# First array carries the per-channel columns; spins in one block; upper 64 partitions on ScalarE's DMA queue

## The chip, the cores and the metric

One core of one Trainium2 chip runs the kernel. The metric is the device time of one launch in microseconds (us): the median of the runs shown. Changes are told in us and as a share of that time.

## What is computed

The reference is one layer of a hybrid encoder on 1024 frames of 1024 channels, all in float32:

```
h = rms_norm(x, norm1_g)
[u | q | k | v] = h @ w_in            (widths 512, 512, 128, 128)
a = pooling mixer(u), scaled by pool_scale
b = sliding-window attention(q, k, v) with q_norm_g, k_norm_g, sinks
x = x + concat(a, b) @ w_out
x = x + squared_relu(rms_norm(x, norm2_g) @ w_up) @ w_down
```

The part that the change touches is the very start: the projection of the first two tiles of 128 frames to k, v and q, which needs `norm1_g` as a scale of the rows of `w_in`.

## The kernel before, in words

**Precision.** Each float32 product is made as three TensorE products of rounded operands: high x high, low x high, high x low. The high part of an operand is its value rounded to fp32r, written by a copy on ScalarE; the low part is the value less the high part, written by a subtraction on VectorE. So nothing can be multiplied before ScalarE has written a high part, and nothing with a low part before VectorE has followed. For the weights both engines multiply by `g1`, the columns of `norm1_g` (one value per partition and k).

**Stages.** The frames are 8 tiles of 128, the 1024 input channels are 8 blocks `k` of 128. The program goes through projections and mixers (to about 180 us), the up projection and the down projection. Each engine has its own list of instructions, written out by hand; semaphores tie them together.

**The start, engine by engine** (line numbers of the profile):

- SP issues the loads. Three arrays come first (L416): `first_0` (tile 0's channels of k = 0, 1, and the k, v weights of k = 0, 1; 128 x 768 words), `first_1` (the same for tile 1, tile 0's k = 2, 3, the weights of k = 2, 3; 128 x 1024), `first_2` (tile 1's k = 2, 3 and the q weights of k = 0; 128 x 768). The q weights of k = 1 to 3 (L355), the second halves of x (L340), and the other k, v weights (L352) follow.
- ScalarE issues one load of its own (L883): `columns`, 18 rows of 128 words, which hold `norm1_g`, `pool_scale`, the q and k gains and the sinks as rows. It makes two slices of the attention bias (L881) and then the high parts in the order of the table `FIRST`: x of tile 0 (L662, `x_first_high`), k, v weights 0 and 1 (L693, `split_w_kv`), x of tile 1 (L662), tile 0's second pair (L666), weights 2 and 3 (L693), tile 1's second pair (L666), q weights 0 to 3 (L698).
- TensorE waits for a tile of zeros, multiplies it with itself 11 times ("spins", L1589: products whose result nobody reads), turns `columns` into 18 columns (L1775, a transpose through the array), spins 5 times, and then goes through the k, v products of k = 0 to 3 (L1581, 24 products of 256 columns, `project_first_kv`), with 2, 2 and 1 spins between them, and the q products (L1619 with high weights, L1623 with low ones, 512 columns each).
- VectorE makes the distance table and four slices of the bias (L1322, L1324), copies the turned columns out of PSUM to `per_row` (L1328), which both engines need as `g1`, and makes the low parts in ScalarE's order (L1055, L1060, L1112).

`first_hi` and `first_lo` count the high and low parts done; `first_count(kind, i)` is the place of a part in `FIRST`.

The list of TensorE at this place is this:

```python
            pe.wait_ge(setup_pool, 1)
            spin(11)
            pe.wait_ge(setup_pool, 4)
            pe.wait_ge(cols_in, 16)
            nc.tensor.transpose(bank[QT_B][:, 0:N_COLS], cols_rows[0:N_COLS, :], ...)
            spin(5)
            project_first_kv()
            project_first_q(range(KH), range(2))
```

Of the kernel before, what the change touches and what calls it, by code (L numbers as in the profile page):

```python
# [8 lines left out]
ACT = mybir.ActivationFunctionType  # L9
# [7 lines left out]
def hybrid_trunk(nc, x, x_T, columns, first_0, first_1, first_2, w_kv, w_q, w_u, pool_w, w_out, norm2_g, w_up, w_down, out):  # L17
# [33 lines left out]
    with ExitStack() as ctx:  # L51
# [100 lines left out]
        per_row = small(N_COLS)  # L152
        g1, pool_sc = per_row[:, 0:KT], per_row[:, KT:KT + GROUPS]
# [45 lines left out]
        cols_in, constants_in, x_tok_in = sem("cols_in"), sem("constants_in"), sem("x_tok_in")  # L199
# [19 lines left out]
        cols_turned = sem("cols_turned")  # L219
# [41 lines left out]
        FIRST = ([("x", 0), ("kv", 0), ("kv", 1), ("x", 1), ("kv", 2), ("kv", 3)] + [("q", k) for k in range(KH)]  # L261
                 + [("kv", k) for k in range(KH, KT)] + [("q", k) for k in range(KH, KT)])

        def first_count(kind, i):

            return FIRST.index((kind, i)) + 1

# [8 lines left out]
        COLS_READY = 1 + PAIRS + 1  # L276

# [60 lines left out]
        def _(sp):  # L338
# [76 lines left out]
            for i, piece in enumerate((first_0, first_1, first_2)):  # L415
                sp.dma_start(first_stage[i], piece).then_inc(first_in[i], 16)  # L416
# [9 lines left out]
            sp.wait_ge(first_lo, first_count("q", 0))  # L426
# [14 lines left out]
            sp.wait_ge(first_lo, len(FIRST))  # L441
# [203 lines left out]
        def _(sc):  # L645
# [14 lines left out]
            def x_first_high(t):  # L660
                sc.wait_ge(first_in[t], 16)
                nc.scalar.activation(act(HI, 0, t)[:, 0:2, :], x_first[t], ACT.Copy).then_inc(first_hi, 1)  # L662
# [60 lines left out]
            def copy_kv(t):  # L723
# [3 lines left out]
                else:  # L727
                    sc.wait_ge(first_lo, len(FIRST))
# [154 lines left out]
            sc.dma_start(cols_rows[0:N_COLS, :], columns).then_inc(cols_in, 16)  # L883
# [168 lines left out]
        def _(dve):  # L1052
            def x_first_low(t):
                dve.wait_ge(first_hi, first_count("x", t))
# [272 lines left out]
            dve.wait_ge(cols_turned, 1)  # L1327
            step(nc.vector.tensor_copy(per_row, bank[QT_B][:, 0:N_COLS]))  # L1328
# [19 lines left out]
            dve.wait_ge(first_lo, len(FIRST))  # L1348
# [196 lines left out]
        def _(pe):  # L1545
# [19 lines left out]
            def first_kv(t, k, x_part, w_part):  # L1565

                if (x_part, w_part) == (HI, HI):
                    if k < 2:
                        pe.wait_ge(first_hi, first_count("x", t))
# [3 lines left out]
                elif x_part == LO:  # L1573
                    if k < 2:
                        pe.wait_ge(first_lo, first_count("x", t))
                    else:
                        pe.wait_ge(xT_lo, xT_count(t, k // KH))
                else:
                    pe.wait_ge(first_lo, first_count("kv", k))
# [422 lines left out]
```

## Time and profile before

| | |
|---|---|
| median of 3 runs | 861.8 us (861.65 to 862.2) |
| the profiled execution, its own time | 862.25 us |
| its span, first to last instruction | 860.4 us |
| TensorE busy in the span | 856.7 us |
| VectorE, ScalarE, GpSimd busy | 541.7, 417.8, 232.1 us |

How to read it: a row of the timeline gives the start of a group of equal instructions, the time from its first start to its last end, the engine (PE is TensorE's matmul, PEld its weight load; DVE is VectorE, ACT ScalarE, POOL GpSimd, SPq and ACTq the engines' DMA issues), the line, the operation with what it writes and reads, and how many there are. Idle time before it and what ended it stand in brackets. Every product has one weight load, and the loads start one after the other at the pace of the products; so the start of one PEld row less that of the row before, by the number of loads in it, is the time of one product. The start of a PE row lies some 0.2 to 0.3 us behind its load.

### The profile page before, as it was taken

What the parts mean: (1) busy time and instruction counts of PE and PEld (TensorE: products, weight loads), DVE (VectorE), ACT (ScalarE), POOL (GpSimd) and SP (SyncE); (2) the same over time, 40 slices, a digit from 0 to 9 for tenths busy, and PEclk for the clock granted to TensorE, in tenths of its full rate; (3) what the DMA queues carried; (4) which work ended last, traced back from release to release, by engine and by line L of the source; (5) the groups of instructions that cost most, each with busy time, mean ns of one, the idle gap of its engine ahead of it and who ended that gap; (6) DMA issues with size and microseconds to landing.
All of it is one profiled execution on the core that took longest, in us unless ns stands there. A gap on an engine that the chain in (4) does not pass through costs nothing.

```text
span 860.4 us, 10823 instructions
## 1 busy us (share of the span) xinstructions
PE 856.7 (100%) x4068; PEld 710.8 (83%) x4068; DVE 541.7 (63%) x750; ACT 417.8 (49%) x737; POOL 232.1 (27%) x194
## 2 busy tenths in 40 slices
PE   9999999999999999999999999999999999999998
PEld 8888888888888888888888888888888888888887
DVE  7788588844477766656666566458745464646463
ACT  8875446632157555555555555534333333333330
POOL 1421202010141222244322223005543004444440
PEclk9999999999999999999999999999999999999999
DMA  9431013651011743355543332899742453342422
GB/s 353 174 107 66 26 26 73 221 196 50 32 42 50 240 165 134 135 177 177 168 153 135 135 136 97 307 373 363 268 167 95 166 190 120 103 138 100 143 98 74
DMA packets 67519, 128.37 MB, mean 149 GB/s; under 512 B 3578, under 2 KB 20236, under 8 KB 67468
## 3 DMA queue, kind: packets, MB, share of 16 engines
q1 hardware_dynamic: 67296, 127.55, 42.6%
q8 instruction: 32, 0.52, 0.2%
q14 instruction: 20, 0.16, 0.1%
q10 hardware_dynamic: 171, 0.14, 0.0%
HBM read 89.92 MB, written 37.75 MB: 148 GB/s over the span
## 4 chain that ended last, share of the span: by engine, by line
PE 100%; DVE 0%; POOL 0%; issue 0%; POOLq 0%
PE bank L1548 31%; PE bank L1549 31%; PE bank L1550 31%; PE bank L1751 1%; PE bank L1767 1%; PE bank L1561 1%; PE bank L1720 1%; PE bank L1619 1%; PE bank L1589 1%; PE bank L1581 1%; PE bank L1700 0%; PE bank L1623 0%; PE bank L1921 0%; PE bank L1926 0%; PE bank L1713 0%; PE bank L1704 0%
## 5 line engine op out<-in xcount | busy, mean ns | idle before, releaser
L1548 PE MATMUL bank<-b_op,s_op 128*128 128x512 f32 x446 | 173.2, 388 | 0.0
L1549 PE MATMUL bank<-b_op,s_op 128*128 128x512 f32 x446 | 173.1, 388 | 0.0
L1550 PE MATMUL bank<-b_op,s_op 128*128 128x512 f32 x446 | 173.1, 388 | 0.0
L1295 DVE TENSOR_TENSOR s_op<-s_in,s_op 128x1024 fp32r<-128x1024 f32 x56 | 74.4, 1329 | 126.9 <-ACT s_op L870 126.8
L634 POOL TENSOR_TENSOR b_sum<-d_raw,d_raw 128x1024 f32<-128x1024 f32 x40 | 96.9, 2422 | 201.1 <-DVE b_op L1299 201.1
L870 ACT ACTIVATE s_op<-s_in 128x1024 fp32r<-128x1024 f32 x56 | 59.4, 1060 | 177.3 <-PE bank L1550 148.8
L1256 DVE TENSOR_TENSOR ring<-raw,ring 128x512 fp32r<-128x512 f32 x96 | 88.3, 934 | 30.7 <-ACT ring L818 29.1
L1548 PE MATMUL bank<-xs,ring 128*128 128x512 f32 x256 | 99.7, 389 | 0.0
L1550 PE MATMUL bank<-xs,ring 128*128 128x512 f32 x256 | 99.6, 389 | 0.0
L1549 PE MATMUL bank<-xs,ring 128*128 128x512 f32 x256 | 99.6, 389 | 0.0
L1548 PEld LDWEIGHTS bank<-b_op,s_op 128*128 128x128 f32 x446 | 83.7, 188 | 17.5 <-DVE b_op L1299 0.3
L1550 PEld LDWEIGHTS bank<-b_op,s_op 128*128 128x128 f32 x446 | 83.7, 188 | 17.4
L1549 PEld LDWEIGHTS bank<-b_op,s_op 128*128 128x128 f32 x446 | 83.7, 188 | 17.1
L1548 PE MATMUL bank<-wgt,xs 128*128 128x512 f32 (+1 forms) x232 | 86.9, 374 | 0.0
L1550 PE MATMUL bank<-wgt,xs 128*128 128x512 f32 (+1 forms) x232 | 85.0, 366 | 0.0
L1549 PE MATMUL bank<-wgt,xs 128*128 128x512 f32 (+1 forms) x232 | 84.9, 366 | 0.0
L1548 PE MATMUL bank<-t_M,ring 128*128 128x512 f32 x192 | 74.7, 389 | 0.0
L1549 PE MATMUL bank<-t_M,ring 128*128 128x512 f32 x192 | 74.7, 389 | 0.0
L1550 PE MATMUL bank<-t_M,ring 128*128 128x512 f32 x192 | 74.7, 389 | 0.0
L593 POOL TENSOR_TENSOR raw<-raw 128x512 f32<-128x512 f32 x16 | 26.6, 1660 | 166.7 <-DVE ring L1256 166.6
L818 ACT ACTIVATE ring<-raw 128x512 fp32r<-128x512 f32 x96 | 59.2, 620 | 23.1 <-POOL raw L593 20.9
L1550 PEld LDWEIGHTS bank<-xs,ring 128*128 128x128 f32 x256 | 48.0, 188 | 10.0
(174 smaller groups left out, 1434.3 us busy)
## 6 DMA issues: line engine op xcount, KB each, us to landing
s_in<-h_keep SPq DMA_DIRECT2D x56, 512.0 KB, 3.8
h_keep<-h_set SPq DMA_DIRECT2D x16, 1280.0 KB, 5.1
raw<-in_w_up SPq DMA_DIRECT2D x16, 1024.0 KB, 5.7
d_raw<-in_w_down SPq DMA_DIRECT2D x32, 512.0 KB, 7.8
mem<-in_x SPq DMA_DIRECT2D x16, 512.0 KB, 5.2
h_keep<-h_set SPq DMA_DIRECT2D x16, 512.0 KB, 4.0
x_keep<-mem SPq DMA_DIRECT2D x8, 512.0 KB, 2.9
mem<-x_keep SPq DMA_DIRECT2D x8, 512.0 KB, 6.3
```

The source lines that it names most:

```text
L593: nc.gpsimd.tensor_tensor(out=w12, in0=w12, in1=w11, op=ALU.subtract).then_inc(w_four_ready, 1)
L634: nc.gpsimd.tensor_tensor(out=b_sum[G % 2], in0=group_rows(qa, g), in1=group_rows(qb, g), op=op).then_inc(b_summed, 1)
L818: nc.scalar.activation(ring[n % 6][:, HI], weight_block(n), ACT.Copy).then_inc(w_hi, 1)
L870: nc.scalar.activation(s_op[G % 3][:, HI], s_in[G % 3], ACT.Copy).then_inc(op_hi, 1)
L1256: nc.vector.tensor_tensor(out=ring[n % 6][:, LO], in0=weight_block(n), in1=ring[n % 6][:, HI].bitcast(F32), op=ALU.subtract).then_inc(w_lo, 1)
L1295: nc.vector.tensor_tensor(out=s_op[G % 3][:, LO], in0=s_in[G % 3], in1=s_op[G % 3][:, HI].bitcast(F32), op=ALU.subtract).then_inc(op_lo, 1)
L1548: nc.tensor.matmul(out_ap, lhs[HI], rhs[HI], start=first, stop=False, skip_group_check=chained)
L1549: nc.tensor.matmul(out_ap, lhs[HI], rhs[LO], start=False, stop=False, skip_group_check=chained)
L1550: return nc.tensor.matmul(out_ap, lhs[LO], rhs[HI], start=False, stop=last, skip_group_check=chained)
L1561: last = nc.tensor.transpose(xt_bank(T, i)[:, k * P:(k + 1) * P], x_norm[:, (4 * i + k) * P:(4 * i + k + 1) * P], ident)
L1581: last = nc.tensor.matmul(bank[KV_B[t]][:, 0:KV_W], act(x_part, k // KH, t)[:, k % KH, :], w_qkv_s[:, k, w_part, KV_COLS], start=k == 0 an ...
L1589: nc.tensor.matmul(bank[OUT_B][:, 0:2 * P], spin_tile[:, 0:P], spin_tile, start=True, stop=True)
```

## The change

The 18 columns come as columns: the host lays them behind the data of `first_0`, in 32 more words per partition (18 used), so that array is 128 x 800 words. The load of `columns`, the transpose and the copy out of PSUM are gone; VectorE copies the staged columns to `per_row` for later use, and the first two weight splits on ScalarE read them where they landed. `first_0` is loaded in two parts: partitions 0 to 63 from SP, 64 to 127 from ScalarE's queue, both counted by `first_in[0]`, now to 32. The high part of tile 0's x moves from ScalarE to VectorE (a copy with rounding, semaphore `x0_first_hi`), so ScalarE begins with the weights. TensorE spins 15 times in one block and not at all between products, and the 24 k, v products and the first q products stand in another order: the loop over k is outside, tile 1's low-x products of k = 2, 3 are put between the q products of k = 0.

```diff
-        cols_rows = view(a_junk + 2 * P, P)
-
-        a_first = [a_A, a_A + 3 * KV_W, a_A + 7 * KV_W]
-        first_stage = [view(a, w) for a, w in zip(a_first, (3 * KV_W, 4 * KV_W, 3 * KV_W))]
+
+        W_FIRST = (3 * KV_W + 32, 4 * KV_W, 3 * KV_W)
+        a_first = [a_A + sum(W_FIRST[:i]) for i in range(3)]
+        first_stage = [view(a, w) for a, w in zip(a_first, W_FIRST)]
...
+        staged_cols = view(a_first[0] + 3 * KV_W, N_COLS)
...
-        FIRST = ([("x", 0), ("kv", 0), ("kv", 1), ("x", 1), ("kv", 2), ("kv", 3)] + [("q", k) for k in range(KH)]
+        FIRST = ([("kv", 0), ("kv", 1), ("x", 1), ("kv", 2), ("kv", 3)] + [("q", k) for k in range(KH)]
...
+            return 1 if (kind, i) == ("x", 0) else first_count(kind, i) + 1
...
+        FIRST_LANDED = 32
...
-            for i, piece in enumerate((first_0, first_1, first_2)):
-                sp.dma_start(first_stage[i], piece).then_inc(first_in[i], 16)
+            sp.dma_start(first_stage[0][0:HD, :], first_0[0:HD, :]).then_inc(first_in[0], 16)
+            sp.dma_start(first_stage[1], first_1).then_inc(first_in[1], 16)
+            sp.dma_start(first_stage[2], first_2).then_inc(first_in[2], 16)
...
-                sc.wait_ge(w_kv_in[k // 2], 16)
+                sc.wait_ge(w_kv_in[k // 2], FIRST_LANDED if k < 2 else 16)
                 nc.scalar.activation(w_qkv_s[:, k, HI, KV_COLS], w_kv_stage[k // 2][:, k % 2, :], ACT.Copy,
-                                     scale=g1[:, k:k + 1]).then_inc(first_hi, 1)
+                                     scale=(staged_cols if k < 2 else g1)[:, k:k + 1]).then_inc(first_hi, 1)
...
-            sc.dma_start(cols_rows[0:N_COLS, :], columns).then_inc(cols_in, 16)
+            sc.dma_start(first_stage[0][HD:P, :], first_0[HD:P, :]).then_inc(first_in[0], 16)
             sc.wait_ge(setup_dve, 1)
             slope_rows(0)
             slope_rows(1)
-            x_first_high(0)
-            sc.wait_ge(setup_dve, COLS_READY)
             for k in range(2):
                 split_w_kv(k)
-            x_first_high(1)
+            x1_first_high()
             x_second_high(0)
+            sc.wait_ge(setup_dve, COLS_READY)
...
-            dve.wait_ge(cols_turned, 1)
-            step(nc.vector.tensor_copy(per_row, bank[QT_B][:, 0:N_COLS]))
+            dve.wait_ge(first_in[0], FIRST_LANDED)
+            nc.vector.tensor_copy(act(HI, 0, 0)[:, 0:2, :], x_first[0]).then_inc(x0_first_hi, 1)
+            step(nc.vector.tensor_copy(per_row, staged_cols))
...
-                first_kv(0, 0, HI, HI)
-                spin(2)
-                first_kv(0, 0, LO, HI)
-                first_kv(0, 1, HI, HI)
-                first_kv(0, 1, LO, HI)
-                spin(2)
-                for k in range(2):
-                    first_kv(0, k, HI, LO)
-                for k in range(2):
-                    first_kv(1, k, HI, HI)
-                for k in range(2):
-                    first_kv(1, k, HI, LO)
-                spin(1)
-                for k in range(2):
-                    first_kv(1, k, LO, HI)
-                for t in range(2):
-                    for x_part, w_part in ((HI, HI), (LO, HI), (HI, LO)):
-                        for k in range(2, KH):
-                            first_kv(t, k, x_part, w_part)
+                def blocks(t, ks, x_part, w_part):
+                    for k in ks:
+                        first_kv(t, k, x_part, w_part)
+
+                blocks(0, range(2), HI, HI)
+                blocks(0, range(2), LO, HI)
+                first_kv(0, 0, HI, LO)
+                blocks(1, range(2), HI, HI)
+                first_kv(0, 1, HI, LO)
+                blocks(1, range(2), HI, LO)
+                blocks(1, range(2), LO, HI)
+                for k in range(2, KH):
+                    first_kv(0, k, HI, HI)
+                    first_kv(0, k, LO, HI)
+                blocks(1, range(2, KH), HI, HI)
+                for k in range(2, KH):
+                    for t in range(2):
+                        first_kv(t, k, HI, LO)
+                first_q_high(0, range(2))
+                blocks(1, range(2, KH), LO, HI)
+                first_q_low(0, range(2))
...
-            spin(11)
+            spin(15)
             pe.wait_ge(setup_pool, 4)
-            pe.wait_ge(cols_in, 16)
-            nc.tensor.transpose(bank[QT_B][:, 0:N_COLS], cols_rows[0:N_COLS, :], ident[0:N_COLS, 0:N_COLS]).then_inc(cols_turned, 1)
-            spin(5)
             project_first_kv()
-            project_first_q(range(KH), range(2))
+            project_first_q(range(1, KH), range(2))
```

`first_q_high` and `first_q_low` are the two halves of the loop body of `project_first_q` before: the four products of a k with high q weights, and the two with low ones.

TensorE at the start of the program, before (`spin_tile` is the tile of zeros, `xs_50` the first half of x's parts, `wgt` the weights' parts):

```order
L1589 MATMUL bank<-spin_tile 128x256 [waits setup_pool]
L1589 MATMUL bank<-spin_tile 128x256 x10
L1775 MATMUL bank<-mem 128x18 [waits cols_in,setup_pool]
L1589 MATMUL bank<-spin_tile 128x256 x5
L1581 MATMUL bank<-wgt,xs_50 128x256 [waits first_hi]
L1589 MATMUL bank<-spin_tile 128x256 x2
L1581 MATMUL bank<-wgt,xs_50 128x256 [waits first_lo]
L1581 MATMUL bank<-wgt,xs_50 128x256 [waits first_hi]
L1581 MATMUL bank<-wgt,xs_50 128x256 [waits first_lo]
L1589 MATMUL bank<-spin_tile 128x256 x2
L1581 MATMUL bank<-wgt,xs_50 128x256 [waits first_lo] x2
L1581 MATMUL bank<-wgt,xs_50 128x256 [waits first_hi] x2
```

TensorE at the same place, with the change:

```order
L1602 MATMUL bank<-spin_tile 128x256 [waits setup_pool]
L1602 MATMUL bank<-spin_tile 128x256 x14
L1594 MATMUL bank<-wgt,xs_50 128x256 [waits first_hi,x0_first_hi,setup_pool]
L1594 MATMUL bank<-wgt,xs_50 128x256 [waits first_hi,x0_first_hi]
L1594 MATMUL bank<-wgt,xs_50 128x256 [waits first_lo] x3
L1594 MATMUL bank<-wgt,xs_50 128x256 [waits first_hi] x2
L1594 MATMUL bank<-wgt,xs_50 128x256 [waits first_lo] x5
L1594 MATMUL bank<-wgt,xs_50 128x256 [waits first_hi,xT_hi]
L1594 MATMUL bank<-wgt,xs_50 128x256 [waits xT_lo]
L1594 MATMUL bank<-wgt,xs_50 128x256 [waits first_hi,xT_hi]
L1594 MATMUL bank<-wgt,xs_50 128x256 [waits xT_lo]
L1594 MATMUL bank<-wgt,xs_50 128x256 [waits first_hi,xT_hi] x2
```

The transpose (128x18) is gone, 15 spins stand together ahead of the first product and none behind it, and the first wait of a product is now for VectorE's rounding (`x0_first_hi`) and ScalarE's (`first_hi`) both.

ScalarE at the start, before (`mem` is the staging memory):

```order
L883 DMA mem<-in_columns 18x128
L881 ACT_TABLE_LOAD
L881 ACTIVATE mem<-mem 64x128 [waits setup_dve]
L881 ACTIVATE mem<-mem 64x128
L662 ACTIVATE xs_50<-mem 128x2x128 [waits first_in0]
L693 ACTIVATE wgt<-mem 128x256 [waits first_in0,setup_dve]
L693 ACTIVATE wgt<-mem 128x256 [waits first_in0]
L662 ACTIVATE xs_50<-mem 128x2x128 [waits first_in1]
L666 ACTIVATE xs_50<-mem 128x2x128 [waits first_in1]
```

ScalarE at the same place, with the change:

```order
L890 DMA mem<-in_first 64x800
L888 ACT_TABLE_LOAD
L888 ACTIVATE mem<-mem 64x128 [waits setup_dve]
L888 ACTIVATE mem<-mem 64x128
L700 ACTIVATE wgt<-mem 128x256 [waits first_in0] x2
L669 ACTIVATE xs_50<-mem 128x2x128 [waits first_in1]
L673 ACTIVATE xs_50<-mem 128x2x128 [waits first_in1]
L700 ACTIVATE wgt<-mem 128x256 [waits first_in1,setup_dve]
```

Its load is now half of `first_0`, its first step behind the bias is a weight split, and the rounding of tile 0's x has left it; on VectorE a CAST 128x2x128 that waits for `first_in0` and a COPY 128x18 stand where the copy out of PSUM stood.

## Rows read from the trace of the kernel before

**Rows 1.** the page, busy time of each engine

```profile
PE 856.7 (100%) x4068; PEld 710.8 (83%) x4068; DVE 541.7 (63%) x750; ACT 417.8 (49%) x737; POOL 232.1 (27%) x194
```

**Rows 2.** the page, shares of the chain that ended last

```profile
PE 100%; DVE 0%; POOL 0%; issue 0%; POOLq 0%
```

**Rows 3.** who waited for whom, over the span, weight loads (us, times, longest)

```profile
PEld bank L1548 <- DVE pooled_odd L1173: 0.4, 1, 0.4
```

**Rows 4.** timeline of the weight loads, 0 to 12 us

```profile
1.08 2.42 PEld L1589 LDWEIGHTS bank<-spin_tile 128*128 128x128 f32 x11 [1.08 <-POOL spin_tile L535]
3.73 0.18 PEld L1775 LDWEIGHTS bank<-mem 18*128 18x128 f32 x1 [0.22 <-POOL mem L549]
3.95 1.14 PEld L1589 LDWEIGHTS bank<-spin_tile 128*128 128x128 f32 x5
4.97 0.33 PEld L1581 LDWEIGHTS bank<-wgt,xs 128*128 128x128 f32 x1
...
5.61 0.76 PEld L1581 LDWEIGHTS bank<-wgt,xs 128*128 128x128 f32 x3
6.25 0.54 PEld L1589 LDWEIGHTS bank<-spin_tile 128*128 128x128 f32 x2
6.68 0.88 PEld L1581 LDWEIGHTS bank<-wgt,xs 128*128 128x128 f32 x6
7.49 0.19 PEld L1589 LDWEIGHTS bank<-spin_tile 128*128 128x128 f32 x1
7.61 1.75 PEld L1581 LDWEIGHTS bank<-wgt,xs 128*128 128x128 f32 x14
9.29 0.78 PEld L1619 LDWEIGHTS bank<-wgt,xs 128*128 128x128 f32 x4
```

**Rows 5.** windows: PE busy (x), PEclk granted clock, DMA share, GB/s

```profile
5.00:6.00 1.00, 1.00 (x6) 1.00 1.02 333
```

**Rows 6.** timeline of ScalarE, 0 to 30 us

```profile
0.72 0.59 ACTq L883 DMA_DIRECT2D mem<-in_columns  x1
...
3.86 0.42 ACT L662 ACTIVATE xs<-mem 128x256 fp32r<-128x256 f32 x1 [0.63 <-DMA mem<-in_first]
4.27 0.91 ACT L693 ACTIVATE wgt<-mem 128x256 fp32r<-128x256 f32 x2
5.13 0.42 ACT L662 ACTIVATE xs<-mem 128x256 fp32r<-128x256 f32 x1
...
6.86 2.76 ACT L698 ACTIVATE wgt<-mem 128x512 fp32r<-128x512 f32 x4
```

**Rows 7.** timeline of VectorE, 0 to 30 us

```profile
2.73 1.20 DVE L1324 TENSOR_SCALAR mem<-mem 64x128 f32<-64x128 f32 x4
...
4.38 0.43 DVE L1055 TENSOR_TENSOR xs<-mem,xs 128x256 fp32r<-128x256 f32 x1
...
18.59 0.23 DVE L1180 COPY mem<-mem 128x128 f32<-128x128 f32 x1 [1.12 <-ACT mem L731]
```

**Rows 8.** line L416, the loads of the three first arrays

```profile
L416 SPq DMA_DIRECT2D mem<-in_first x3: 379/417/424, 0.7 to 1.6; - x3
...
DMA to landing us min/median/max: 3.1/4.0/4.7
```

**Rows 9.** issues of `w_out`: L371 in parts of 64 partitions, L366 whole

```profile
L371 SPq DMA_DIRECT2D mem<-in_w_out x8: 465/594/597, 127.4 to 153.0; - x8
L366 SPq DMA_DIRECT2D mem<-in_w_out x4: 328/328/431, 63.1 to 123.5; - x4
```

**Rows 10.** timeline of all engines, 17 to 27 us

```profile
18.01 0.48 ACT L731 ACTIVATE mem<-bank,mem 128x256 f32<-128x256 f32 x1 [1.09 <-POOL mem L557]
...
19.25 0.69 ACT L737 ACTIVATE mem<-bank,mem 128x512 f32<-128x512 f32 x1 [0.77 <-PE bank L1623]
...
24.63 0.82 DVE L1192 TENSOR_TENSOR mem<-mem 128x640 f32<-128x640 f32 x1 [0.54 <-POOL mem L574]
...
26.11 0.60 PE L1700 MATMUL bank<-mem 128*128 128x128 f32 x4
```

More of the change, by code:

```diff
@@ L14, with hybrid_trunk @@
 HI, LO = 0, 1
-def hybrid_trunk(nc, x, x_T, columns, first_0, first_1, first_2, w_kv, w_q, w_u, pool_w, w_out, norm2_g, w_up, w_down, out):
+def hybrid_trunk(nc, x, x_T, first_0, first_1, first_2, w_kv, w_q, w_u, pool_w, w_out, norm2_g, w_up, w_down, out):
     SEQ, D = x.shape[1], x.shape[2]
@@ L1053, in x_first_low @@
             def x_first_low(t):
[L1054 removed]
+                if t == 0:
+                    dve.wait_ge(x0_first_hi, 1)
+                else:
+                    dve.wait_ge(first_hi, first_count("x", 1))
                 nc.vector.tensor_tensor(out=act(LO, 0, t)[:, 0:2, :], in0=x_first[t],
@@ L1568, in first_kv @@
                     if k < 2:
-                        pe.wait_ge(first_hi, first_count("x", t))
+                        if t == 0:
+                            pe.wait_ge(x0_first_hi, 1)
+                        else:
+                            pe.wait_ge(first_hi, first_count("x", 1))
                     else:
@@ new lines, in project_first_kv, with first_q_high @@
+                first_q_high(0, range(2))
+                blocks(1, range(2, KH), LO, HI)
+                first_q_low(0, range(2))
+            def first_q_high(k, tiles):
+                pe.wait_ge(first_hi, first_count("q", k))
+                for t in tiles:
+                    for part in (HI, LO):
+                        nc.tensor.matmul(bank[Q_B[t]][:, :], act(part, k // KH, t)[:, k % KH, :],
+                                         w_qkv_s[:, k, HI, Q_COLS], start=k == 0 and part == HI, stop=False)
@@ L1613, in project_first_q, with first_q_low @@
+            def first_q_low(k, tiles):
+                pe.wait_ge(first_lo, first_lo_count("q", k))
+                for t in tiles:
+                    last = nc.tensor.matmul(bank[Q_B[t]][:, :], act(HI, k // KH, t)[:, k % KH, :],
+                                            w_qkv_s[:, k, LO, Q_COLS], start=False, stop=k == KT - 1)
+                    if k == KT - 1:
+                        last.then_inc(q_done, 1)
             def project_first_q(ks, tiles):
                 for k in ks:
-                    pe.wait_ge(first_hi, first_count("q", k))
@@ L1617, in project_first_q @@
-                    for t in tiles:
-                        for part in (HI, LO):
-                            nc.tensor.matmul(bank[Q_B[t]][:, :], act(part, k // KH, t)[:, k % KH, :],
-                                             w_qkv_s[:, k, HI, Q_COLS], start=k == 0 and part == HI, stop=False)
-                    pe.wait_ge(first_lo, first_count("q", k))
-                    for t in tiles:
-                        last = nc.tensor.matmul(bank[Q_B[t]][:, :], act(HI, k // KH, t)[:, k % KH, :],
-                                                w_qkv_s[:, k, LO, Q_COLS], start=False, stop=k == KT - 1)
-                        if k == KT - 1:
-                            last.then_inc(q_done, 1)
+                    first_q_high(k, tiles)
@@ L1961, in _ @@
                     down(p, g)
-_INS = ["x", "x_T", "columns", "first_0", "first_1", "first_2", "w_kv", "w_q", "w_u", "pool_w", "w_out", "norm2_g", "w_up", "w_down"]
+_INS = ["x", "x_T", "first_0", "first_1", "first_2", "w_kv", "w_q", "w_u", "pool_w", "w_out", "norm2_g", "w_up", "w_down"]
 def kernel(**inputs):
@@ L1987 @@
     laid["pool_w"] = np.asarray(inputs["pool_w"]).transpose(0, 2, 1, 3)[0]
-    laid["columns"] = np.concatenate(
+    columns = np.concatenate(
         [np.asarray(inputs["norm1_g"]).reshape(-1, P).T, np.asarray(inputs["pool_scale"]).reshape(-1, P).T,
          twice(inputs["q_norm_g"]), twice(inputs["k_norm_g"]),
-         np.concatenate([np.tile(sinks[i::2], (P // 2, 1)) for i in range(2)])], axis=1).T
+         np.concatenate([np.tile(sinks[i::2], (P // 2, 1)) for i in range(2)])], axis=1)
+    spare = np.zeros((P, 32 - columns.shape[1]), columns.dtype)
+    laid["first_0"] = np.concatenate([x_pair[0, :, 0], w_kv[0], columns, spare], axis=1)
     arrays, args = {}, []
```

25 lines of the change are left out of this document (13 added, 12 removed).

## The prediction

> **What bounds the kernel now.** I read the page first. TensorE is busy for 856.7 of 860.4 us [rows 1], and the chain that ended last is all TensorE [rows 2]. Behind the start its weight loads wait for another engine for 0.4 us at the longest, over the whole span [rows 3]. So the time is the moment at which TensorE begins, the sum of its instructions, and a short tail. Every instruction taken from its list, and every microsecond by which it gets through the list sooner, moves the end, as long as the operands keep up. Nothing of what ScalarE, VectorE or the DMA save counts by itself.
>
> The second view is the timeline of the weight loads in the first 12 us [rows 4]. It shows what can be saved. The first spin loads at 1.08. Eleven loads end at 3.50, the transpose loads at 3.73, the next spins at 3.95, and the first real product only at 4.97. Then 2 spins, 3 products, 2 spins, 6 products, 1 spin, 14 products; the q products begin at 9.29. The pace changes on the way: 3 loads from 5.61 to 6.25 are 0.213 us each, 14 from 7.61 to 9.29 are 0.120 us. From 6.68 to 7.49 there are 6: one of 0.21 and five of 0.12. The granted clock of the profile reads 1.00 in this stretch already [rows 5], but 256 columns in 0.213 us are the 1.2 GHz level, and 0.120 is possible only at the 2.4 GHz level. So the array changes level at about 6.9 us, having been fed without a hole since 3.95. Before that an instruction costs 0.214, behind it 0.120.
>
> The third views are the operands' engines [rows 6, 7]. ScalarE stands idle for 0.63 us and begins the high part of tile 0's x at 3.86, when `first_0` is in: the shortest way from issue to landing is 3.1 us from 0.7, so 3.8 [rows 8]. The two weight splits run from 4.27, 0.43 apart. The next step is at 5.13, and `first_1`, issued one issue of 0.42 us later with 4.0 us to landing [rows 8], comes at the same moment: from there on ScalarE is tied to the data or to its own work, until the q weights from 6.86.
>
> **The change, part by part.**
>
> *The list of TensorE.* 21 spins become 15 and the transpose goes. Eleven loads from 1.08 with 0.214 between them put a twelfth at about 3.40, where before the next spin came at 3.95: the transpose and the holes around it cost 0.55 us. With the first gap 0.16 as in the trace, 15 spins hand over at 1.08 + 0.16 + 14 x 0.214 = 4.24.
>
> *When the first product can start.* It needs two parts. VectorE's four bias slices end at 3.93 [rows 7], just behind the landing at 3.8, so its rounding of 128 x 256 starts at 3.93. The trace has no such copy on VectorE. Its bounds are 0.23, the copy of half that size, and 0.43, the subtraction of the same size [rows 7]; I take 0.36, nearer the upper one since the destination is rounded too, so 4.29. ScalarE, freed of x, starts its first weight split at 3.86 instead of 4.27 and ends it 0.48 later, at 4.34. With 0.06 for the semaphore the first product loads at 4.40, against 4.97. VectorE's copy matters only if it is over 0.4 us.
>
> *The products up to the change of level.* The second product waits for weights 1, 4.34 + 0.43 + 0.06 = 4.83, an idle of 0.22. Then VectorE's chain: `per_row` copy to about 4.45, low x to 4.88, low weights 0 to 5.32, 1 to 5.76 (0.44 each), low x of tile 1 to 6.14. High x of tile 1 is there at 5.13 + 0.42 + 0.06 = 5.61, bound by `first_1` and so not earlier than before. At 0.214 the products load at 4.40, 4.83, 5.05, 5.26, 5.47 (low weights 0, 5.38: in time), 5.69 (tile 1: 5.61, in time), 5.90, 6.11 (low weights 1, 5.82), 6.33, 6.54, 6.76 (low x of tile 1, 6.20). If the level changes at 6.9 as before, the thirteenth loads at 7.05. Before it loaded at 7.61 + 2 x 0.12 = 7.85. That is **0.80 us**, and it is the whole term. It is smaller than the 1.75 us taken out (0.55 of hole, 5 slow spins of 0.214, one fast of 0.12), because 1.63 of them lie before the change of level: real products take their place at the slow pace, and a product done early saves only what it would have cost later, 0.120.
>
> *Behind it.* Does TensorE, 0.8 us early, now catch up with its operands? ScalarE's and VectorE's lists from `first_1` on are what they were. The closest are: high x of tile 1, k = 2, 3, in before 7.0, wanted at 7.5; low weights 3, ready near 7.3, wanted at 8.0; high q weights 0, ready at 6.86 + 0.72 = 7.6, wanted at 8.2. The low x products that would come too soon are those that the new order puts behind the first q products. The q weights follow at 0.70 us per k on both engines, TensorE needs 1.36 us per k, so its margin grows. Farther on one chain does not move: ScalarE takes k, v of tile 0 at 18.01, behind GpSimd. But its copy of q waited 0.77 us for TensorE, starts at 18.49 instead of 19.25, and carries the chain to VectorE's 24.63 + 0.82 = 25.45 with it, 0.76 us earlier; the transpose that needs it moves from 26.11 to 25.3, and finds it 0.6 us before [rows 10]. I carry the 0.80 to the end.
>
> *The DMAs.* Bytes: 16 KB more in `first_0`, 9 KB of `columns` less, no cost beside the 1.28 MB of the three arrays. ScalarE's issue of `columns` took 0.59 us [rows 6], and its half of `first_0` stands in the same slot; the idle of 0.63 ahead of 3.86 covers a longer one. On SP issues by 64 partitions took 0.594 where whole ones took 0.328 [rows 9], so `first_1` may be issued up to 0.27 us later; its packets queue behind those of `first_0` anyway. Does the split bring the landing forward? An earlier landing than 3.8 is worth next to nothing, since VectorE comes at 3.93. A later one costs up to its own length, less the 0.1 that VectorE gives. The Trainium skill (DMA: Bandwidth & Descriptors, "Issuing engines are not separate DMA queues") says that loads started by different engines run on the same 16 DMA engines, and that only the time to issue is saved. By it the landing stays at 3.8 and the sum stays as it is; no row before has a load split so, and the rule speaks against this part of the change, not for a loss.
>
> **The sum.** The profiled execution took 862.25 us with a span of 860.4; with 0.80 less these are 861.45 and 859.6. The median of the runs, 861.8, lies 0.45 under the profiled one; I take the 0.80 from it: **861.0 us**. What a measurement of this kernel can tell from no change is about 0.2%, or 1.7 us, and the forecast is inside it.
>
> **The rivals.**
>
> *The fast level comes earlier.* Before, TensorE ran from 1.08 with a hole at 3.5 to 3.95 and rose at 6.9; with the hole gone it might rise before. For it: the hole is the only thing between the first spin and the rise. Against it: the operands bound the first products, so fast products would wait. The last part, high q weights 0 at 7.67, then limits: q products from 7.7 instead of 9.29 less the four of tile 1 or k moved behind them (2 x 0.12), which gives 9.29 - 0.24 - 7.7 = 1.35 of gain at most: 860.5 us. The Trainium skill (TensorE: Matmul & The Clock Gate, Part 1, "What's actually happening") calls the slow clock the resting state that activity releases. By that rule an unbroken block of spins should help, and this trace agrees as far as it rises only after a long stretch of work.
>
> *The fast level comes later: slower than before.* The spins between products covered waits; now TensorE stands idle for 0.22 us ahead of the second product, and for more if an operand is late, still on the slow level. If such holes put off the rise, each microsecond at the slow level costs 1 - 0.120/0.214 = 0.44 us. The gain of 0.80 is gone when the rise comes 1.8 us later, at 8.7. If it came a whole stretch like 3.95 to 6.9 later, at 9.8, the cost is 1.28 and the kernel is 0.5 us slower: 862.3. For it: 4 spins stood just there. Against it: before, TensorE rose with a hole of half a microsecond only 3 us back, and the new holes sum to less. The same rule of the skill, read the other way, is this rival's.
>
> *The upper half lands late.* ScalarE's half comes through the other queue, while SP's queue already sends `first_1` on the same DMA engines. If it lands at 4.6, the first product loads at 5.2 instead of 4.40, with some slack retaken from the later products: about 0.35 us of gain is left, 861.5. If the landing is at 5.0, nothing is left: 861.8.
>
> *The gain is lost behind.* A wait that is covered now by under 0.8 us could take it back in the mixers; the one of 0.4 us [rows 3] shows that some are close. The time would be 861.5 to 861.8. Against it: every chain that I followed starts from TensorE.
>
> **How the numbers follow.** The forecast has 0.55, the earlier rise 0.13, the late half 0.12, the gain lost behind 0.10, the later rise 0.10. The forecast's own range is 860.5 to 861.5, with the 0.3 us by which runs of one kernel differ to either side. For 8 in 10 I go down to 860.0 (the earlier rise, a run's spread lower) and up to 862.0 (most of the late rise and little else lie beyond). Faster by over 0.2% needs 860.1 or less, the lower end of the earlier rise and what I do not see: 0.09. Slower by over 0.2% needs 863.5, beyond the late rise: 0.04. Within 0.2%: 0.87.
>
> **What would show it.** In the timeline of the changed kernel: 15 spin loads from 1.08 to about 4.24; the first product's load at 4.4; ScalarE's first split at 3.86 and its first use of `first_1` at 5.13 again; loads 0.214 apart up to 6.9 and 0.120 behind; the first q product's load at about 8.2; the transposes of 26.11 at 25.3. A first wait on a DMA past 4.0 would mean the late half, fast loads before 6.5 the earlier rise, slow ones past 7.2 the later one. A span over 860.4 with all of this in place would make the forecast wrong: something behind took the gain.

## The result: slower, and the profile after

| | before | after |
|---|---|---|
| median | 862.19 us (22 runs) | 863.51 us (22 runs) |
| lowest and highest run | 861.4 to 862.9 | 862.03 to 864.86 |
| span of the profiled execution | 860.4 us | 861.7 us |

The ratio of the runs is 1.0014, with a 95% interval of 1.0009 to 1.002: slower by 1.3 us, where 0.8 us less was forecast. The time lies above the range. Two things in the table matter beside the median: the kernel before is at 862.19 over 22 runs and not at the 861.8 of its first three, and the runs of the changed kernel spread over 2.8 us instead of 1.5.

The page, busy time of each engine, after:

```profile
PE 856.8 (99%) x4061; PEld 710.9 (82%) x4061; DVE 536.1 (62%) x751; ACT 416.0 (48%) x736; POOL 233.6 (27%) x194
```

TensorE's work is the same as before within 0.1 us [rows 1]; what grew is the time in which it does none. The timeline of its weight loads shows where (answers to [rows 4]):

```profile
1.08 3.27 PEld L1602 LDWEIGHTS bank<-spin_tile 128*128 128x128 f32 x15 [1.08 <-POOL spin_tile L542]
5.85 4.57 PEld L1594 LDWEIGHTS bank<-wgt,xs 128*128 128x128 f32 x22 [1.50 <-issue]
10.35 0.77 PEld L1632 LDWEIGHTS bank<-wgt,xs 128*128 128x128 f32 x4
```

The 15 spins are where they were expected. The first product then loads at 5.85 instead of the 4.40 forecast, behind a hole of 1.5 us, and the 22 products take 4.50 us, 0.205 each: the slow pace nearly to the end, since the loads come closer only from 9.9 on. The q products begin at 10.35 with 22 products done, before at 9.29 with 24. Counting the two at 0.120, TensorE is 1.30 us late here. The last product of the program:

```profile
858.80 0.28 PE L1560 MATMUL bank<-b_op,s_op 128*128 128x256 f32 x1
```

Before, its counterpart started at 857.49: 1.31 us. So what is lost by 10 us is what is lost at the end; nothing in between gives or takes. The timelines of ScalarE and VectorE (answer to [rows 6, 7]) show what the first product waited for:

```profile
0.73 0.58 ACTq L890 DMA_DIRECT2D mem<-in_first  x1
...
5.23 0.91 ACT L700 ACTIVATE wgt<-mem 128x256 fp32r<-128x256 f32 x2 [2.00 <-DMA mem<-in_first]
```

```profile
2.73 1.20 DVE L1333 TENSOR_SCALAR mem<-mem 64x128 f32<-64x128 f32 x4
5.23 0.29 DVE L1337 CAST xs<-mem 128x256 fp32r<-128x256 f32 x1 [1.30 <-DMA mem<-in_first]
```

Both stand idle up to 5.23 and are released by the same load. `first_1` is first used at 6.27. By line, the two halves and `first_1`, time from issue to landing (answer to [rows 8]):

```profile
L421 SPq DMA_DIRECT2D mem<-in_first x1: 560/560/560, 0.7 to 0.7; - x1
...
DMA to landing us min/median/max: 3.4/3.4/3.4
```

```profile
L890 ACTq DMA_DIRECT2D mem<-in_first x1: 581/581/581, 0.7 to 0.7; - x1
...
DMA to landing us min/median/max: 4.5/4.5/4.5
```

```profile
DMA to landing us min/median/max: 4.9/4.9/4.9
```

SP's half lands at 4.1, ScalarE's at 5.2. The whole array landed at 3.8. Both halves are issued at 0.7, but in the trace the packets of SP's half start at 2.06 and those of ScalarE's only at 2.92; before, the packets of the whole array started at 1.73. Below is what the DMA engines move in 5 us, 40 slices of 0.125 us, after and before:

```profile
GB/s 0 0 0 0 0 0 0 0 0 0 0 0 0 0 0 0 179 154 102 51 230 307 230 102 102 102 231 282 366 307 413 369 445 255 197 197 262 229 295 262
```

```profile
GB/s 0 1 0 0 0 0 0 0 0 0 0 0 0 156 184 74 98 25 221 127 295 319 393 418 451 442 410 393 459 459 393 393 393 459 451 393 402 369 393 393
```

Before, the data starts at 1.6 us and runs near 400 GB/s from 2.75 on. After, it starts at 2.0, has two slow stretches (51 to 102 GB/s at 2.25 to 2.5 and 102 at 2.9 to 3.25), reaches 400 at 3.75 and falls to 197 again at 4.25. At the 5.2 us at which ScalarE can start, the kernel before had had `first_1` as well.

### The profile page after: what moved, and what is told of

Read it like the earlier page. It is cut to its first block, busy times and chain, and to the rows that moved or that the text cites. A ratio compares the mean times of both kernels' runs of the same rounds, so it can differ in the third digit from the quotient of the medians.

```text
span 861.7 us, 10808 instructions
## 1 busy us (share of the span) xinstructions
PE 856.8 (99%) x4061; PEld 710.9 (82%) x4061; DVE 536.1 (62%) x751; ACT 416.0 (48%) x736; POOL 233.6 (27%) x194
## 4 chain that ended last, share of the span: by engine, by line
PE 99%; DMA 1%; ACT 0%; DVE 0%; issue 0%
PE bank L1558 31%; PE bank L1560 31%; PE bank L1559 31%; PE bank L1771 1%; PE bank L1787 1%; PE bank L1571 1%; PE bank L1740 1%; PE bank L1594 1%; PE bank L1632 1%; DMA mem<-in_first 1%; PE bank L1720 0%; PE bank L1638 0%; PE bank L1938 0%; PE bank L1943 0%; PE bank L1733 0%; PE bank L1724 0%
## 5 line engine op out<-in xcount | busy, mean ns | idle before, releaser
L1304 DVE TENSOR_TENSOR s_op<-s_in,s_op 128x1024 fp32r<-128x1024 f32 x56 | 76.5, 1366 | 124.8 <-ACT s_op L877 124.8
L1265 DVE TENSOR_TENSOR ring<-raw,ring 128x512 fp32r<-128x512 f32 x96 | 86.5, 915 | 40.0 <-ACT ring L825 39.2
L600 POOL TENSOR_TENSOR raw<-raw 128x512 f32<-128x512 f32 x16 | 29.6, 1850 | 165.2 <-DVE ring L1265 165.1
```

Of the source, the lines that this page charges most:

```text
L600: nc.gpsimd.tensor_tensor(out=w12, in0=w12, in1=w11, op=ALU.subtract).then_inc(w_four_ready, 1)
L1265: nc.vector.tensor_tensor(out=ring[n % 6][:, LO], in0=weight_block(n), in1=ring[n % 6][:, HI].bitcast(F32), op=ALU.subtract).then_inc(w_lo, 1)
L1304: nc.vector.tensor_tensor(out=s_op[G % 3][:, LO], in0=s_in[G % 3], in1=s_op[G % 3][:, HI].bitcast(F32), op=ALU.subtract).then_inc(op_lo, 1)
```

## The experiments

Two causes had to be told apart, and each could be the other's cover. **Theory A**: the load in two halves is late. **Theory A1**: the hole that it makes on TensorE puts off the fast level. The rivals: the missing spins between products (B), a slow memory start that has nothing to do with the split (C). Medians stand beside the kernel before on the same chip.

### The first array whole again (e1_whole_sp)

```diff
-            sp.dma_start(first_stage[0][0:HD, :], first_0[0:HD, :]).then_inc(first_in[0], 16)
+            sp.dma_start(first_stage[0], first_0).then_inc(first_in[0], 16)
...
-            sc.dma_start(first_stage[0][HD:P, :], first_0[HD:P, :]).then_inc(first_in[0], 16)
...
-        FIRST_LANDED = 32
+        FIRST_LANDED = 16
```

> The changed kernel with first_0 loaded whole, by one transfer from SP, and ScalarE's queue without a load. Theory A (the loss is the load in two halves: ScalarE's half starts its packets at 2.92 us and lands at 5.2): the array lands near 3.9, the first product's load is at 4.4 to 4.5, the array goes to the fast level near 6.9, and the time is 0.8 us under the kernel before and 2.1 under the changed one. Rival B (the loss is the missing cover of spins between the products, which puts off the fast level to 9.9): the first product is as early, but the fast level still comes near 10, and the time is about 0.5 us above the kernel before. Rival C (the late landing is the memory's slow start and not the split): landing past 4.8, time as the changed kernel's.

Measured: 861.69 us (861.26 to 863.16, 11 runs), before 862.16 (30 runs). One transfer in place of two takes 1.8 us off the changed kernel. Its weight loads, and ScalarE:

```profile
1.08 3.28 PEld L1601 LDWEIGHTS bank<-spin_tile 128*128 128x128 f32 x15 [1.08 <-POOL spin_tile L542]
4.49 1.01 PEld L1593 LDWEIGHTS bank<-wgt,xs 128*128 128x128 f32 x5
6.63 2.19 PEld L1593 LDWEIGHTS bank<-wgt,xs 128*128 128x128 f32 x17 [1.13 <-ACT xs L669]
8.75 0.78 PEld L1631 LDWEIGHTS bank<-wgt,xs 128*128 128x128 f32 x4
```

```profile
3.87 0.91 ACT L700 ACTIVATE wgt<-mem 128x256 fp32r<-128x256 f32 x2 [0.63 <-DMA mem<-in_first]
6.17 0.42 ACT L669 ACTIVATE xs<-mem 128x256 fp32r<-128x256 f32 x1 [1.39 <-DMA mem<-in_first]
```

The array lands as before, and the first product loads at 4.49, where 4.40 was forecast. Behind the hole the 17 products take 2.12 us, 0.125 each, so the fast level is there by 6.6, with no spin between the products. Theory A holds; B and C fall. But the fall against before is 0.47 and not 0.80: `first_1` came at 6.17 in this execution, and TensorE stood idle for 1.1 us ahead of tile 1. Nine of the 11 runs lie at 861.26 to 861.97, two at 863.15.

### The hole filled, the halves left (e2_spin22)

```diff
-            spin(15)
+            spin(22)
```

> The changed kernel with 22 spins in the block instead of 15, so that TensorE has work up to 5.74 us and the hole of 1.5 us ahead of the first product is filled; both halves land at 5.2 as before. Theory A1 (the hole on the slow level puts off the fast level): the fast level comes near 6.9 and not at 9.9, the 24 products take some 3 us instead of 4.6, and the time is 1.2 us under the changed kernel, near the kernel before. Rival (the moment of the fast level has nothing to do with the hole): it stays near 9.9 and the time is the changed kernel's, within 0.2.

Measured: 862.36 us (861.97 to 862.55, 11 runs), before 862.16: 1.15 us under the changed kernel, with a spread of 0.6 us instead of 2.8.

```profile
4.77 0.91 ACT L700 ACTIVATE wgt<-mem 128x256 fp32r<-128x256 f32 x2 [1.53 <-DMA mem<-in_first]
```

```profile
1.08 4.77 PEld L1602 LDWEIGHTS bank<-spin_tile 128*128 128x128 f32 x22 [1.08 <-POOL spin_tile L542]
5.73 3.19 PEld L1594 LDWEIGHTS bank<-wgt,xs 128*128 128x128 f32 x22
8.85 0.78 PEld L1632 LDWEIGHTS bank<-wgt,xs 128*128 128x128 f32 x4
```

The late half lands at 4.77 in this trace and not at 5.2, but the spins hold TensorE until 5.73, so the first product is no earlier in effect (5.73, after 5.85). The 22 products take 3.12 us instead of 4.50. Seven spins more, work that nobody reads, save 1.15 us. The granted clock's column reads 1.00 at the start of this trace as of the others; it is the pace that tells. Theory A1 holds.

### Both halves from SP (e3_halves_sp), and the whole from ScalarE (e4_whole_act)

```diff
             sp.dma_start(first_stage[0][0:HD, :], first_0[0:HD, :]).then_inc(first_in[0], 16)
+            sp.dma_start(first_stage[0][HD:P, :], first_0[HD:P, :]).then_inc(first_in[0], 16)
...
-            sc.dma_start(first_stage[0][HD:P, :], first_0[HD:P, :]).then_inc(first_in[0], 16)
```

> The changed kernel with both halves of first_0 issued by SP, one behind the other, and ScalarE without a load. If it is the second queue that makes the upper half late, the halves land near 4.3, which is 0.2 to 0.4 behind a whole load for the second issue of 0.56 us, and the time is about 0.5 us under the kernel before. If it is the transfer by 64 partitions that is slow, whoever issues it, the second half lands near 5 and the time is near the changed kernel's.

Measured: 863.96 us (863.38 to 865.97, 8 runs), before 862.16. The half issued second by SP:

```profile
L422 SPq DMA_DIRECT2D mem<-in_first x1: 575/575/575, 1.3 to 1.3; - x1
...
DMA to landing us min/median/max: 3.5/3.5/3.5
```

From 1.3 it lands at 4.8, with one queue only, near the 5 of the second case. So the array in halves is late on either queue, and the second queue is not needed for it. The size of the transfer explains little: from issue to landing this half takes 3.5 us and the one ahead of it 3.2, where the whole array took 3.1 to 3.5 in six traces. Half the array takes as long as the whole of it. What makes the second half late here is that it is issued 0.6 us later. In the changed kernel it is issued at 0.7, and that is lost again: on ScalarE's queue it takes 4.0 to 4.5 us in three traces.

Here `first_1` is later too, and TensorE has two holes. The weight loads around the second one, then windows of 1 us, where the column behind PE's busy time is the granted clock:

```profile
5.93 0.53 PEld L1594 LDWEIGHTS bank<-wgt,xs 128*128 128x128 f32 x4 [0.21 <-issue]
7.60 3.52 PEld L1594 LDWEIGHTS bank<-wgt,xs 128*128 128x128 f32 x17 [1.14 <-ACT xs L670]
```

```profile
4.00:5.00 1.00, 0.44 (x4) 1.00 1.04 266
5.00:6.00 1.00, 0.40 (x2) 1.00 0.83 273
6.00:7.00 1.00, 0.67 (x4) 1.00 0.73 259
7.00:8.00 1.00, 0.40 (x2) 0.73 0.85 298
8.00:9.00 1.00, 1.00 (x6) 0.50 1.06 405
9.00:10.00 1.00, 1.00 (x7) 0.50 1.05 404
10.00:11.00 1.00, 1.00 (x7) 0.57 1.06 410
11.00:12.00 1.00, 1.00 (x7) 1.00 1.05 399
```

The four loads from 5.93 start 0.11 apart, so the fast level had been reached by then. TensorE, busy for 0.40 to 0.67 of each microsecond from 4 to 7, falls to half the clock, the 1.2 GHz level, at 7 to 8, and with full work from 8 on comes back only at 10 to 11. The 17 loads from 7.60 to 11.05 are 0.203 apart. This is the one trace in which the profile's clock column itself shows the level change near the start.

The opposite case, the array whole but on ScalarE's queue while SP begins with `first_1`:

```diff
-            sp.dma_start(first_stage[0][0:HD, :], first_0[0:HD, :]).then_inc(first_in[0], 16)
...
-            sc.dma_start(first_stage[0][HD:P, :], first_0[HD:P, :]).then_inc(first_in[0], 16)
+            sc.dma_start(first_stage[0], first_0).then_inc(first_in[0], 16)
```

(`FIRST_LANDED` is 16 here as well.)

> The changed kernel with first_0 whole, issued by ScalarE, while SP begins with first_1. If transfers of two queues share the engines and hold each other up, first_0 lands past 5 us, mixed with first_1, and the time is that of the changed kernel or above it. If the queue of ScalarE is as good as SP's and only the split costs, it lands near 4 and first_1 is earlier too, for a time at least 0.8 us under the kernel before.

Measured: 863.70 us (862.11 to 865.37, 11 runs), before 862.16.

```profile
L889 ACTq DMA_DIRECT2D mem<-in_first x1: 403/403/403, 0.7 to 0.7; - x1
...
DMA to landing us min/median/max: 4.7/4.7/4.7
```

It is issued in 0.40 us and lands 4.7 us later, at 5.4. Its packets run from 2.12 to 5.04, those of `first_1` on SP's queue from 1.72 to 4.79: the array that is wanted first comes in step with the one that is wanted second. The Trainium skill (DMA: Bandwidth & Descriptors, "Issuing engines are not separate DMA queues") says that such loads interleave on the same 16 engines; these overlapping stretches agree.

### The split alone, in the kernel before (e6_before_split)

```diff
-            for i, piece in enumerate((first_0, first_1, first_2)):
-                sp.dma_start(first_stage[i], piece).then_inc(first_in[i], 16)
+            sp.dma_start(first_stage[0][0:HD, :], first_0[0:HD, :]).then_inc(first_in[0], 16)
+            sp.dma_start(first_stage[1], first_1).then_inc(first_in[1], 16)
+            sp.dma_start(first_stage[2], first_2).then_inc(first_in[2], 16)
...
-                sc.wait_ge(first_in[t], 16)
+                sc.wait_ge(first_in[t], 32 if t == 0 else 16)
...
-                sc.wait_ge(w_kv_in[k // 2], 16)
+                sc.wait_ge(w_kv_in[k // 2], 32 if k < 2 else 16)
...
             sc.dma_start(cols_rows[0:N_COLS, :], columns).then_inc(cols_in, 16)
+            sc.dma_start(first_stage[0][HD:P, :], first_0[HD:P, :]).then_inc(first_in[0], 16)
```

> The kernel before with the load of first_0 alone split (lower 64 partitions from SP, upper 64 from ScalarE's queue behind columns); spins, order and columns as before. Theory A (the split is the loss): the array lands past 5 instead of 3.8, the first product loads near 6.0 instead of 4.97, and the time is 0.6 to 1.6 us above the kernel before. Rival (the split costs only together with the new list, whose spins end at 4.2): the list of before absorbs it, and the time is within 0.3 us of before.

Measured: 865.32 us (864.62 to 866.09, 5 runs), before 862.15: 3.2 us slower, twice what was expected at the most. The half is issued at 1.36 here, behind the columns, and lands at 6.3.

```profile
3.94 1.14 PEld L1591 LDWEIGHTS bank<-spin_tile 128*128 128x128 f32 x5
7.27 0.29 PEld L1583 LDWEIGHTS bank<-wgt,xs 128*128 128x128 f32 x1 [2.19 <-ACT wgt L694]
7.44 0.55 PEld L1591 LDWEIGHTS bank<-spin_tile 128*128 128x128 f32 x2
...
8.94 1.40 PEld L1583 LDWEIGHTS bank<-wgt,xs 128*128 128x128 f32 x6
10.22 0.33 PEld L1591 LDWEIGHTS bank<-spin_tile 128*128 128x128 f32 x1
```

The hole is 2.2 us, and six products from 8.94 to 10.22 still take 0.213 us each. The spins of the list of before stand behind the wait, where they cover nothing. This run shows that the split alone makes the kernel slower; its size does not carry over to the changed kernel, since the half is issued 0.6 us later here.

### The old order of the products, the rest of the change kept (e7_whole_oldlist)

```diff
             def project_first_kv():
...
                first_kv(0, 0, HI, HI)
+                spin(2)
                first_kv(0, 0, LO, HI)
...
-            project_first_q(range(1, KH), range(2))
+            project_first_q(range(KH), range(2))
```

(with the load of e1_whole_sp, and the whole of `project_first_kv` as in the kernel before; the rounding on VectorE and the block of 15 spins stay)

> The columns in the first array alone: first_0 whole from SP with the columns behind its data, no transpose, rounding of tile 0 on VectorE, 15 spins in one block, but the products in the order of the kernel before with its 2, 2 and 1 spins between them. If the early start of the products is the gain and the order of the products only keeps them fed, the time lies between before and e1_whole_sp: 0.1 to 0.5 us under before, and no long runs. If the gain of e1_whole_sp comes from the removed spins, it is the time of before.

Measured: 861.67 us (861.3 to 862.4, 11 runs), before 862.15: 0.48 us less, as e1_whole_sp, and no long run.

```profile
4.94 0.31 PEld L1601 LDWEIGHTS bank<-spin_tile 128*128 128x128 f32 x2
8.33 0.78 PEld L1629 LDWEIGHTS bank<-wgt,xs 128*128 128x128 f32 x4
```

What the change gains is in the part that this kernel keeps, the columns in the first array and the earlier start. The new order and the spins removed between the products add nothing that the medians show. The profiled execution is the fastest, 861.3 us: the two spins from 4.94 to 5.18 are 0.12 us each, so the fast level was there already, and the q products begin at 8.33, 0.96 earlier than in the first trace of the kernel before.

### Cover for the second array (e5_whole_cover)

```diff
                 first_kv(0, 0, HI, LO)
+                spin(4)
                 blocks(1, range(2), HI, HI)
```

(on top of e1_whole_sp)

> The changed kernel with first_0 whole from SP (as in e1_whole_sp) and 4 spins put back ahead of tile 1's first product, where e1_whole_sp stood idle for over 1 us because first_1 came at 6.2. Theory A1 (a hole on the slow level can put off the fast level by a whole step, and did so in the two of 11 runs of e1_whole_sp that took 863.15 instead of 861.3 to 861.9): no run of this kernel is above 862.3, and the median is that of e1_whole_sp or up to 0.3 above it, since the 4 spins cost up to 0.5 us where first_1 is in time. Rival (the two long runs have another cause): long runs come as often as in e1_whole_sp.

Measured: 861.71 us (861.3 to 862.59, 11 runs). The median is that of e1_whole_sp and the runs at 863.15 are gone, but the highest, at 862.59, is above the 862.3 that was expected, and 2 of 11 against 0 of 11 is few to tell from chance. That run is the profiled one: its products stand 0.14 us earlier than those of the kernel before at 30 us and 0.29 later at 80, so 0.43 us were lost between. The trace shows where:

```profile
30.35 1.06 ACT L657 ACTIVATE mem<-mem 128x1024 f32<-128x1024 f32 x1 [1.02 <-DMA mem<-in_x]
33.56 0.19 PEld L1557 LDWEIGHTS bank<-xs,wgt 128*128 128x128 f32 x1 [0.51 <-DVE xs L1074]
```

ScalarE waits 1.02 us for a load of x (0.18 in the kernel before), its rounding and VectorE's low part follow later, and TensorE waits 0.51 us for that low part. Why that load came late in this execution was not tested.

### A hole with no late data (e8_hole)

```diff
-            spin(15)
+            spin(8)
```

(on top of e1_whole_sp)

> e1_whole_sp (first_0 whole, landing at 3.9, products from 4.5) with 8 spins instead of 15: TensorE does nothing between 2.7 and 4.5 us, a hole as long as the one that the late half makes in the changed kernel, but here no operand is late. Theory A1 (a hole on the slow level puts off the fast level in most executions): the median rises by 0.8 to 1.5 us over e1_whole_sp, to 862.5 to 863.2, with runs spread over 2 us, and the fast level comes after 7. Rival (the hole is harmless, and the changed kernel pays for late data alone): 861.7, within 0.2.

Measured: 862.57 us (862.19 to 863.81, 11 runs), 0.9 above e1_whole_sp. Its lowest run is above nine of the 11 of e1_whole_sp.

```profile
1.08 1.78 PEld L1601 LDWEIGHTS bank<-spin_tile 128*128 128x128 f32 x8 [1.08 <-POOL spin_tile L542]
4.84 4.95 PEld L1593 LDWEIGHTS bank<-wgt,xs 128*128 128x128 f32 x22 [1.98 <-issue]
9.68 1.34 PEld L1631 LDWEIGHTS bank<-wgt,xs 128*128 128x128 f32 x4
```

TensorE is idle from 2.9 to 4.8, and 22 products take 4.84 us, 0.22 each with the waits, at the slow pace to the end. No operand waits for a spin, so the seven that are gone can have delayed nothing but the fast level. A hole on TensorE alone costs 0.9 us, which settles A1. The array landed at 4.2 in this execution, 0.3 later than in that of e1_whole_sp; where the first product came 1.24 us later without a hole (e2_spin22) the cost was 0.67, so 0.3 are worth an estimated 0.2.

### Second traces of both kernels (before_look, after_look)

> The kernel before, once more, for a second trace of its loads. If the landing of first_1 at 5.1 to 5.2 us belongs to the kernel, it comes there again within 0.2 us, and the later landings with first_0 of 3200 bytes per partition (5.4, 5.75 and 6.2) are the change's. If it varies by itself from execution to execution, it may come anywhere from 5.1 to 6.2 here too.

> The changed kernel, once more, for a second trace. Theory A: ScalarE's half lands between 4.7 and 5.3 again, a full microsecond behind the 3.8 of the whole load, and TensorE stands idle ahead of its first product for over 0.5 us; the moment of the fast level may be another than 9.9. Rival: 5.2 was one bad execution and the half lands by 4.3.

ScalarE in the kernel before, then ScalarE and the weight loads in the changed one:

```profile
4.10 0.42 ACT L662 ACTIVATE xs<-mem 128x256 fp32r<-128x256 f32 x1 [0.87 <-DMA mem<-in_first]
...
5.34 0.42 ACT L662 ACTIVATE xs<-mem 128x256 fp32r<-128x256 f32 x1
```

```profile
5.02 0.91 ACT L700 ACTIVATE wgt<-mem 128x256 fp32r<-128x256 f32 x2 [1.79 <-DMA mem<-in_first]
6.09 0.42 ACT L669 ACTIVATE xs<-mem 128x256 fp32r<-128x256 f32 x1 [0.16 <-DMA mem<-in_first]
```

```profile
5.64 0.19 PEld L1594 LDWEIGHTS bank<-wgt,xs 128*128 128x128 f32 x1 [1.29 <-issue]
6.04 2.70 PEld L1594 LDWEIGHTS bank<-wgt,xs 128*128 128x128 f32 x21 [0.21 <-issue]
8.67 0.78 PEld L1632 LDWEIGHTS bank<-wgt,xs 128*128 128x128 f32 x4
```

The kernel before took 863.11 us in its execution, with `first_0` in at 4.1 and `first_1` used at 5.34, so both can move by a few tenths. Its q products begin at 9.67 instead of 9.29; that is 0.38 us of the 0.86 between the two executions, and the rest came up behind 180 us and was not followed. The late half shows again in the changed kernel (5.02), and `first_1` again near 6.1. Yet this execution took 861.97 us: the 21 products from 6.04 take 2.63 us, 0.125 each, so the fast level was there by 6.0, in spite of the hole. The same list, the same late half, and 1.5 us between two executions: that is the spread of the changed kernel's runs. The moment of the rise varies from execution to execution, and the hole shifts its odds.

All twelve traces bear that out, read by the pace of the loads and by the clock changes that the traces record. In the six without a hole of over half a microsecond ahead of the first product, the fast level came at 6.9 and 7.7 (the kernel before), 5.1 (e1_whole_sp), 6.7 (e2_spin22), 7.2 (e5_whole_cover) and by 4.9 (e7_whole_oldlist). In the six with a hole of 1.3 to 2.2 us there it came at 9.9 (the changed kernel), 10.3 (e4_whole_act), 10.5 (e6_before_split) and 10.9 (e8_hole), but by 6.0 in after_look and e3_halves_sp. So the hole does not always put it off; in four of six traces it did, and without a hole none came after 7.7.

## Why the prediction was wrong

- **The first product at 4.40.** It failed in one step, the paragraph on the DMAs: "By it the landing stays at 3.8 and the sum stays as it is". I put it at 3.8 for halves whose issues the rows already priced: 0.594 for 64 partitions against 0.328. The later half lands at 5.2, 5.0 and 4.8 (the changed kernel twice, e2_spin22), the whole array at 3.8 to 4.2 in six traces. With the array whole the product loads at 4.49 (e1_whole_sp): the rest of that step was right.
- **The rounding on VectorE** takes 0.29, between the bounds of 0.23 and 0.43; I took 0.36. It decides nothing.
- **The hole ahead of the first product.** The sum had spins to 4.24 and a product at 4.40, so no hole; it was 1.5 us, by the landing above. (The idle of 0.22 that the prediction names stands ahead of the second product and came as forecast, 0.21 in after_look.) That hole carries both of the large terms of the miss, since the rivals were priced apart. "The upper half lands late" was given 861.8 at a landing of 5.0, with nothing added for the clock; "the fast level comes later" was given 862.3, with the words "the new holes sum to less". The first can bring on the second. The runs price both: the late data costs 0.67 us with the hole filled (e2_spin22 less e1_whole_sp), and the hole 1.15 us (the changed kernel less e2_spin22). The 0.67 is rather too much for the late data alone: in the trace of e2_spin22 the spins go on for an estimated 0.3 us after its data would have let a product start.
- **The prices of the rivals** agree with the runs within their spread. A first product later by 1.2 us at 0.120/0.214 = 0.56 for each costs 0.67, and 0.67 was measured; by that the prediction should have left 0.13 us of gain at a landing of 5.0 and not nothing. The 1.28 for a rise at 9.8 stands beside 1.15 and 0.9 (e8_hole).
- **The gain of 0.80.** It is 0.47 (e1_whole_sp) or 0.48 (e7_whole_oldlist), with intervals that take in 0. The term was sized against one execution with the rise at 6.9 and `first_1` at 5.13. In the traces of the kernels with the whole load `first_1` was used at 5.4 to 6.2 instead. Whether the longer rows of `first_0` or chance did that, two traces of the kernel before (5.13, 5.34) cannot say.
- **The sum over the parts**: -0.47 for the change without the split, +0.67 for the late data, +1.15 for the hole, together +1.35, against +1.32 measured. This is no test: the three are steps along one chain of runs and must add up to their ends. The test of the largest is e8_hole, which makes a hole another way and costs 0.9. Each is a difference of medians of 11 to 30 runs and, by their spread, uncertain by some 0.4 us or more.
- **"I carry the 0.80 to the end."** Right in kind: 1.30 us at the first q product, 1.31 at the last product of the program.
- **The base.** The forecast started from 861.8, three runs; over 22 the kernel before has 862.19. That alone takes 0.4 of the miss of 2.5 us.

Open: why a transfer of 64 partitions is no faster than one of 128 with twice the bytes, and why on ScalarE's queue it takes some 0.9 us more. Its issue is longer by 0.15 to 0.18 us and its first data comes 0.3 later; the rest was seen and not explained. The whole array is late on ScalarE's queue too, 4.7 us from its issue (e4_whole_act), so the sharing with `first_1` is a likelier reason than the 64 partitions, but the late start of the packets (2.92, where there it was 2.12) is not explained by it. And what decides the moment of the rise within one list; the traces show only that it varies.

## What to carry over

Put what is wanted first into one transfer on one queue, over all 128 partitions; in these runs neither two halves nor a second queue beside it brought it in sooner, and each made it later by half a microsecond or more. Ahead of the first real product, spins should last until the latest landing that occurs, not the usual one: four more between the products cost nothing measurable here, seven fewer ahead of them cost 0.9 us. And when two rivals of a forecast are a late operand and a slow clock, price them together, because the first can cause the second.

## What was not expected

A program can be made faster by products that nobody reads, by 1.15 us for seven spins (e2_spin22), and slower by leaving seven out, by 0.9 us (e8_hole). And the level, once up, can fall again within the first microseconds even with TensorE busy for half of the time: to 0.50 at 8 us in e3_halves_sp. The Trainium skill (TensorE: Matmul & The Clock Gate, Part 1, "What's actually happening") describes the slow clock as the resting state which activity lifts; these traces agree.
